# Last feed-forward fed with the un-normalised stream: the factor 1/rms on its gate and up products, the shift as two more moving columns

## The reference

```python
D_MODEL, SEQ, CTX_LEN, DEPTH, D_FF = 1024, 256, 256, 2, 2816

def _rms(x, w):
    return x * lax.rsqrt(jnp.mean(x * x, axis=-1, keepdims=True) + EPS) * w

def _modulate(x, shift, scale):
    return x * (1 + scale[:, None, :]) + shift[:, None, :]

def _swiglu(x, w_gu, w_down):
    g, u = jnp.split(x @ w_gu, 2, axis=-1)
    return (jax.nn.silu(g) * u) @ w_down

for l in range(DEPTH):
    ...
    h = h + 0.5 * m[2][:, None] * _swiglu(_modulate(_rms(h, norm_w[l, 0]), m[0], m[1]), ffn1_w_gu[l], ffn1_w_down[l])
    ...
    h = h + m[5][:, None] * y          # y: the mixer's output
    h = h + 0.5 * m[8][:, None] * _swiglu(_modulate(_rms(h, norm_w[l, 2]), m[6], m[7]), ffn2_w_gu[l], ffn2_w_down[l])
return h                               # the latent stream alone
```

## Time and profile before

| | |
|---|---|
| median of 3 runs | 1715.92 us (1715.57 to 1716.11) |
| the profiled execution, its own time | 1716.46 us |
| its span on the core | 1714.7 us |
| TensorE matmul busy | 1664.4 us, 97% |
| VectorE busy | 1085.4 us, 63% |
| ScalarE busy | 609.5 us, 36% |
| mean granted TensorE clock | 0.993 |

### The profile page before, as it was taken

One profiled execution on the slowest core, in us unless ns is written; L12 is line 12 of the kernel. 1 busy time (PEld: TensorE's weight loads), 2 busy tenths in 40 slices (PEclk: granted clock), 3 DMA queues, 4 the chain that ended last, 5 costly groups with the idle time before them and its releaser, 6 DMA issues.

```text
span 1714.7 us, 23714 instructions
## 1 busy us (share of the span) xinstructions
PE 1664.4 (97%) x9475; PEld 1412.5 (82%) x9475; DVE 1085.4 (63%) x1652; ACT 609.5 (36%) x917; POOL 85.0 (5%) x150
## 2 busy tenths in 40 slices
PE   3999999999999999999999999999999999979999
PEld 1888888889767898888888898888888987979999
DVE  2777787636668567777773368777523587655543
ACT  2422222124645452222222252222222365444432
POOL 0000000000000100000000000000000000000000
PEclk9999999999999999999999999999999999989999
DMA  9255555532211224555552235555323232435554
GB/s 365 96 187 190 180 195 179 191 111 75 99 62 50 87 87 163 183 195 179 190 188 97 83 101 195 183 185 187 134 97 98 87 111 74 139 116 182 183 169 148
DMA packets 69882, 249.42 MB, mean 145 GB/s; under 512 B 7441, under 2 KB 8465, under 8 KB 69777
## 3 DMA queue, kind: packets, MB, share of 16 engines
q1 hardware_dynamic: 51344, 180.83, 31.7%
q0 software_dynamic: 18432, 67.12, 11.7%
HBM read 246.87 MB, written 1.05 MB: 145 GB/s over the span
## 4 chain that ended last, share of the span: by engine, by line
PE 93%; DVE 2%; DMA 1%; SPq 1%; issue 1%; ACT 1%; POOLq 0%; POOL 0%; DVEq 0%; ACTq 0%
PE ps L1168 30%; PE ps L1169 29%; PE ps L1170 29%; DMA raw<-wstream 1%; PE ps L1229 1%; PE ps L1371 1%; PE ps L1403 1%; ACT whi L398 1%; PE ps L1331 1%; DVE wlo L685 1%; SPq L328 1%; SPq L324 0%; PE ps L1385 0%; DVE nmax L1013 0%; PE ps L1412 0%
## 5 line engine op out<-in xcount | busy, mean ns | idle before, releaser
L685 DVE TENSOR_TENSOR wlo<-raw,whi 128x1024 fp32r<-128x1024 f32 x320 | 393.7, 1230 | 546.8 <-ACT whi L398 545.9
L1168 PE MATMUL ps<-xh,whi 128*128 128x512 f32 (+1 forms) x1956 | 690.2, 353 | 8.5 <-DVE xl L795 5.1
L1169 PE MATMUL ps<-xl,whi 128*128 128x512 f32 (+1 forms) x1956 | 674.3, 345 | 0.0
L1170 PE MATMUL ps<-xh,wlo 128*128 128x512 f32 (+1 forms) x1956 | 673.7, 344 | 0.0
L398 ACT ACTIVATE whi<-raw 128x1024 fp32r<-128x1024 f32 x320 | 338.6, 1058 | 897.5 <-PE ps L1170 764.2
L1168 PEld LDWEIGHTS ps<-xh,whi 128*128 128x128 f32 x1956 | 372.3, 190 | 65.7 <-issue 12.0
L1169 PEld LDWEIGHTS ps<-xl,whi 128*128 128x128 f32 x1956 | 372.6, 190 | 45.7 <-issue 3.8
L1170 PEld LDWEIGHTS ps<-xh,wlo 128*128 128x128 f32 x1956 | 372.2, 190 | 44.7
L710 DVE SCALAR_TENSOR_TENSOR shared_a<-wm,cs,shared_a 128x512 f32<-128x512 f32 x448 | 307.6, 747 | 0.0
L1168 PE MATMUL ps<-ah,whi 128*128 128x512 f32 (+1 forms) x800 | 274.9, 344 | 3.7 <-DVE shared_b L733 3.7
L1169 PE MATMUL ps<-al,whi 128*128 128x512 f32 (+1 forms) x800 | 273.0, 341 | 0.0
(11 more groups left out here) (106 smaller groups left out, 797.5 us busy)
## 6 DMA issues: line engine op xcount, KB each, us to landing
raw<-wstream SPq DMA_DIRECT2D x320, 512.0 KB, 3.5
wm<-wmod POOLq DMA_DIRECT2D x128, 512.0 KB, 4.7
wm<-wmod SPq DMA_DIRECT2D x3, 2048.0 KB, 21.0
h<-x_t SPq DMA_DIRECT2D x1, 2048.0 KB, 11.9
wm<-wmod SPq DMA_DIRECT2D x2, 1024.0 KB, 20.4
out_t<-h SPq DMA_DIRECT2D x8, 128.0 KB, 2.6
K<-cols SPq DMA_DIRECT2D x1, 939.0 KB, 13.8
K<-cols SPq DMA_DIRECT2D x1, 268.5 KB, 3.0
```

The costliest lines, as they stand in the source:

```text
L685: dve.tensor_tensor(wlo[:, n % RING, :, :].rearrange("p a b -> p (a b)"), raw[:, n % RING, :], whi[:, n % SPL, :, :].rearrange("p a b -> p ...
L1168: pe.matmul(out_ap, hi_w, hi_x, start=start, stop=False)
L1169: pe.matmul(out_ap, hi_w, lo_x, start=False, stop=False)
L1170: return pe.matmul(out_ap, lo_w, hi_x, start=False, stop=stop)
```

## The change

Only the last feed-forward and what feeds it change. Since rms^-1 is one factor per token, (x * a * r + s) W = r * (x * a) W + s W. So:

- ScalarE and VectorE make the high and low part of `h * acol`, without the norm's factor, chunk by chunk as the output projection's chunks are added to `h` (`high_last`, `low_last`). They are stored in rows of 512 fp32 (2048 bytes) where the attention's buffers were (`xh_last`, `xl_last`), and columns 256 and 257 of each row hold the shift (of the latent and of the context stream; only the first is used).
- Gate and up matmuls move 258 columns instead of 256. Their first three blocks go chunk by chunk together, with the sum of squares (`norm_stat`) ahead of the last chunk.
- Per hidden chunk ScalarE copies the two shift products out of PSUM (`srow`), VectorE multiplies gate and up by rms^-1 into SBUF in one instruction of 2x256 (`gu_last`, semaphore `gu_scaled`), ScalarE takes silu with the shift product as bias, and VectorE does (up + shift product) * silu. TensorE may overwrite the banks after `gu_scaled`.
- The first half of the down blocks uses banks 4, 6, 7, 5, the second half banks 0 to 3.
- In the output projection VectorE does the update ahead of the split of weights, and the last split of it after `low_last`.

```diff
+XW = S + 2
...
+        rstd_last = shared_b[:, T + S:2 * T]
+        gu_last = af[:, :, S:T]
...
+        xh_last = ah[:, 0:DC * T].rearrange("p (c t) -> p c t", c=DC)
+        xl_last = ah[:, DC * T:2 * DC * T].rearrange("p (c t) -> p c t", c=DC)
+        ah_last = al[:, FC * S:2 * FC * S]
+        al_last = al[:, 0:FC * S]
...
+            def high_last(d):
+                act.wait_ge(h_done, h_count(4, d, 0))
+                act.activation(xh_last[:, d, 0:S], h[:, d, 0:S], ACT.Identity, scale=acol[:, 5, d, 0:1]).then_inc(ha_hi, 1)
+
+            def ffn_last():
...
+                for j in range(FC):
+                    split_next(n0 + 2 * j)
+                    if j:
+                        hidden_high(f, j - 1, w)
+                    b = 2 * j % 4
+                    act.wait_ge(block_done, n0 + 2 * j + 2)
+                    if j >= 2:
+                        act.wait_ge(mul_done, F0 + j - 1)
+                    act.activation(srow[:, j % 2, :, 0:1], ps[:, b:b + 2, S:S + 1], ACT.Copy).then_inc(srow_done, 1)
+                    split_next(n0 + 2 * j + 1)
+                    act.wait_ge(gu_scaled, j + 1)
+                    act.wait_ge(srow_done, j + 1)
+                    act.wait_ge(mul_done, F0 + j - 1)
+                    act.activation(sil[:, j % 2, 0:w], gu_last[:, 0, :], ACT.Silu, bias=srow[:, j % 2, 0, 0:1])\
+                        .then_inc(silu_done, 1)
...
-                    for d in range(JOINT, DC):
-                        split_next(n0 + OQ + d)
-                        square(m, d)
-                    root(m, 0)
+                    for d in range(DC):
+                        split_next(n0 + OQ + d)
+                        high_last(d)
+                        square(m, d)
...
             # VectorE
+            def low_last(d):
+                dve.wait_ge(ha_hi, d + 1)
+                dve.scalar_tensor_tensor(xl_last[:, d, 0:S], h[:, d, 0:S], acol[:, 5, d, 0:1],
+                                         xh_last[:, d, 0:S].bitcast(F32), ALU.mult, ALU.subtract).then_inc(ha_lo, 1)
...
+                    split_next(n0 + 2 * j)
+                    if j:
+                        hidden_low(f, j - 1, w)
...
+                    dve.wait_ge(srow_done, j + 1)
+                    dve.tensor_tensor(gu_last, ps[:, b:b + 2, 0:S], rows, ALU.mult).then_inc(gu_scaled, 1)
+                    split_next(n0 + 2 * j + 1)
+                    dve.wait_ge(gu_scaled, j + 1)
+                    dve.wait_ge(silu_done, F0 + j + 1)
+                    dve.scalar_tensor_tensor(af[:, j % 2, 0:w], gu_last[:, 1, :], srow[:, j % 2, 1, 0:1],
+                                             sil[:, j % 2, 0:w], ALU.add, ALU.mult).then_inc(mul_done, 1)
...
+                for d in range(DC):
+                    dve.wait_ge(block_done, n0 + OQ + d + 1)
+                    update(m, d, d % 4)
+                    if d:
+                        low_last(d - 1)
+                        add_square(m + 1, d - 1)
+                    if d < DC - 1:
+                        split_next(n0 + OQ + d)
+                low_last(DC - 1)
+                split_next(n0 + OQ + DC - 1)
...
             # TensorE
+                for q in range(FIRST):
+                    pe.wait_ge(lo_done, n0 + q + 1)
+                for c in range(DC):
+                    if c == DC - 1:
+                        norm_stat(m)
+                    pe.wait_ge(ha_lo, c + 1)
+                    if c == 0:
+                        pe.wait_ge(h_done, h_count(4, JOINT + FIRST - 1, 0))
+                    for q in range(FIRST):
+                        ins = chunk_last(n0 + q, q, c)
...
+                for b in range(FIRST, GU):
+                    if b % 2 == 0:
+                        pe.wait_ge(gu_scaled, b // 2 - 1)
+                    pe.wait_ge(lo_done, n0 + b + 1)
+                    for c in range(DC):
+                        ins = chunk_last(n0 + b, b % 4, c)
```

More of the change, by code:

```diff
@@ L431, in ffn @@
                     split_next(n0 + GU + b)
[L432 to L435, removed]
+                for d in range(JOINT):
+                    square(m + 1, d)
+                ln_exp_tables()
                 nd = n0 + GU + HALF
@@ L438, in ffn @@
                     split_next(nd + b)
[L439 to L443, removed]
+                boundary(m + 1, nd + HALF)
+            def high_last(d):
+                act.wait_ge(h_done, h_count(4, d, 0))
+                act.activation(xh_last[:, d, 0:S], h[:, d, 0:S], ACT.Identity, scale=acol[:, 5, d, 0:1]).then_inc(ha_hi, 1)
+            def ffn_last():
+                f, w = 3, S
+                F0 = FC * f
+                n0 = PER_LAYER + FFN + MIX
+                for j in range(FC):
[13 more added lines that the diff above has]
+                        .then_inc(silu_done, 1)
+                hidden_high(f, FC - 1, w)
+                for b in range(DN - TAIL):
+                    split_next(n0 + GU + b)
             def ln_exp_tables():
@@ L738, in hidden_low @@
                 dve.wait_ge(ah_done, FC * f + j + 1)
-                dst = slice(j * T, j * T + w)
-                dve.tensor_tensor(al[:, dst], af[:, j % 2, 0:w], ah[:, dst].bitcast(F32), ALU.subtract)\
-                    .then_inc(al_done, 1)
+                dst = slice(j * T, j * T + w) if f < 3 else slice(j * w, (j + 1) * w)
+                high, low = (ah[:, dst], al[:, dst]) if f < 3 else (ah_last[:, dst], al_last[:, dst])
+                dve.tensor_tensor(low, af[:, j % 2, 0:w], high.bitcast(F32), ALU.subtract).then_inc(al_done, 1)
             def gate_columns(m):
@@ L892, in ffn @@
                     split_next(nd + b)
[L893 to L904, removed]
+                dve.wait_ge(block_done, nd + HALF - TAIL)
@@ L1203, in first_blocks, with chunk_last, ffn_last, down @@
                     column_block(n + 2, FIRST_BANKS[m][2], a, b, last)
+            def chunk_last(n, bank, c):
+                return three(ps[:, bank, 0:XW], whi[:, n % SPL, c, :], wlo[:, n % RING, c, :],
+                             xh_last[:, c, 0:XW], xl_last[:, c, 0:XW], c == 0, c == DC - 1)
+            def ffn_last():
+                f, m, w = 3, 5, S
+                n0 = PER_LAYER + FFN + MIX
+                pe.wait_ge(shift_lo, 1)
+                for q in range(FIRST):
[8 more added lines that the diff above has]
+                        ins = chunk_last(n0 + q, q, c)
+                        if c == DC - 1:
+                            ins.then_inc(block_done, 1)
+                pe.wait_ge(h_done, h_count(4, DC - 1, 0))
+                for b in range(FIRST, GU):
[4 more added lines that the diff above has]
+                        ins = chunk_last(n0 + b, b % 4, c)
+                    ins.then_inc(block_done, 1)
+                def down(hf, b, order, parts=0):
+                    n = n0 + GU + HALF * hf + b
+                    banks = DN_BANKS[1 - hf]
+                    pe.wait_ge(lo_done, n + 1)
+                    for r, d in order:
+                        src = (2 * b + r) * w
+                        ins = three(ps[:, banks[d], 0:w], whi[:, n % SPL, 4 * r + d, :],
+                                    wlo[:, n % RING, 4 * r + d, :], ah_last[:, src:src + w], al_last[:, src:src + w],
+                                    b == 0 and r == 0, b == HALF - 1 and r == 1)
+                        if r == 1 and d < parts:
+                            ins.then_inc(part_done, 1)
+                    ins.then_inc(block_done, 1)
+                by_row = [(r, d) for r in range(2) for d in range(4)]
+                by_bank = [(r, d) for d in range(4) for r in range(2)]
+                pe.wait_ge(rstd_done, 2 * m + 1)
+                for b in range(HALF):
+                    pe.wait_ge(al_done, FC * f + 2 * b + 2)
+                    down(0, b, by_row)
+                pe.wait_ge(gu_scaled, FC)
+                for b in range(HALF - 1):
+                    down(1, b, by_row)
+                down(1, HALF - 1, by_bank, parts=3)
@@ L1299, in ffn @@
                     pe.wait_ge(mod_rows, f + 1)
[L1300 to L1304, removed]
                 main = HALF - TAIL
```

93 lines of the change are left out of this document (67 added, 26 removed).

## The result

The changed kernel takes 1705.98 us, median of 4 runs (1704.70 to 1706.85), against 1715.77 before; ratio 0.9942, 95% interval 0.993 to 0.9955. That is 9.8 us less where 17 were forecast, and 2.5 us above the range.

What follows compares the result with a forecast made beforehand. TensorE, busy 97% of the span, was taken as the bound. Of 20.6 us lost there, new losses of 1.3 + 0.7 + 0.7 + 0.9 = 3.6 leave 17.0 less: 1699.2 us forecast, range 1696.2 to 1703.5.

Steps and rivals of the forecast that it cites:

- signs of being wrong: 258-column matmuls more than 2 ns from 256-column ones, shared_b as releaser chunk after chunk, or a low clock behind 1502.
- Start of the feed-forward: Behind the last output projection: TensorE stops 1.2 us instead of 12.6, waiting for weight block 256, and restarts 0.1 slower.
- The sum of squares: Now inside the matmul stream ahead of the last chunk: costs 0.7 us; no slow clock expected, gain 2.7.
- First reuse of banks: Ahead of blocks 258 and 260: waits of 0.3 and 0.2 us, with two restarts 0.7 in all, against 1.0 before.
- Two columns more: Gate/up matmuls of 258 columns: 0.83 ns more each on a line from 256 to 512, 0.9 us over 1056.
- Steady gate/up: Per hidden chunk VectorE needs 3.9 us and ScalarE about 2.9, hidden behind TensorE's 5.8: no cost.
- The rival of a dearer width: Gate/up: 258 columns cost far more than two columns; charged as 32 more 1712.5 us, chance 0.03; slower (1754), 0.05.
- The rival of a chain at every chunk: Gate/up: scaling makes VectorE and ScalarE a chain TensorE waits for each chunk; +10 us, 1709; chance 0.05.
- Down: Between gate/up and down: the 2.6 us stop and the slow clock's 1.6 go; the later half costs 0.
- Rivals 3 and 4: Stop ahead of down stays, 1703.5 us, chance 0.05; start waits longer because splits come late, 1703, chance 0.10.

Runs made afterwards that it cites:

- gap128_in_before: The kernel before with only an unused tile of 128 bytes a partition added ahead of shared_a; 1720.56 us, ratio 1.0031.
- srow_no_shift: The changed kernel with srow as a piece of the dead tile mrows, so every other buffer lies as in the kernel before; 1699.96 us, ratio 0.9908.
- no_shift_256_columns: As srow_no_shift, but gate and up matmuls move 256 columns, shift products left out and column 0 read in their place; 1698.49 us, ratio 0.9903.
- banks_swapped_in_before: The kernel before with only the last feed-forward's down blocks taking banks 4, 6, 7, 5 first, 0 to 3 later; 1711.78 us, ratio 0.9977.
- update_first_in_before: The kernel before with only VectorE's update of h ahead of the weight split in the last output projection, last split behind the norm; 1708.19 us, ratio 0.996.

## Why the prediction was wrong

**The step that failed** is none of the terms, but what stood under them: that outside the listed parts the kernel stays as it is. "From the profiled execution 1716.46 - 17.0" carries all that stands ahead of 1501 over unchanged, as does "I set SyncE's issues up to 1501.4 as before": a cost put at nothing, without a reason. The new tile `srow` moved `ah` and `al` against the weights by 128 bytes, and 1296 matmuls of 512 columns in the three earlier down stretches cost 5.6 to 6.1 ns more each. With what the 256-column ones of these stretches give back that is 7.1 us. The full diff has it (`srow = sb(...)` ahead of `shared_a`), the lines of it that I showed leave it out, and no rival of mine had it. gap128_in_before shows the cause with nothing else changed, and srow_no_shift that the rest of the sum holds: 1700.0 for 1699.2. Of the signs of being wrong that the prediction names, one came: 258 columns are 2.2 ns dearer than the 120.0 of 256 before, and 3.5 dearer than the 118.7 of 256 beside them. It pointed at the columns, which are not where most of the miss lay.

Point by point, in the changed kernel:

- *Start of the feed-forward*: 1.2 us and a restart were forecast, set by weight block 256. The row of 1508.46 names `wlo` as releaser and the gap is 1.23 us (1507.23 to 1508.46). Right; part of it is the chance of one execution, since the gap is 1.47 in srow_no_shift and 0.7 to 1.5 in the four kernels made from it, with the same order of work.
- *The sum of squares*: 0.68 us from 1516.23 to 1516.91. Right. The clock stayed at 1.00.
- *First reuse of banks*: 0.7 us forecast for two stops; they were 0.1 each with 0.1 for each restart, 0.4. The first scaling is ready at 1521.1 and the second at 1527.2, which are the 1514.9 to 1515.1 and the 1521.1 worked out plus the 6.0. The chains were sized right; TensorE itself came 0.2 to 0.3 later to both, in part because its 258-column matmuls were dearer, and so waited less. In srow_no_shift the second stop is 0.46. Right in place, small in size. The two scalings on VectorE, and ScalarE ahead of the second:

```profile
1520.42 0.68 DVE L965 TENSOR_TENSOR shared_b<-ps,shared_b 128x512 f32<-128x512 f32 x1
1526.47 0.69 DVE L965 TENSOR_TENSOR shared_b<-ps,shared_b 128x512 f32<-128x512 f32 x1
...
1521.13 1.06 ACT L414 ACTIVATE whi<-raw 128x1024 fp32r<-128x1024 f32 x1 [1.90 <-DMA raw<-wstream]
1522.21 1.28 ACT L480 ACT_TABLE_LOAD   x1
1523.51 0.51 ACT L480 ACTIVATE shared_b<-shared_b,srow 128x256 f32<-128x256 f32 x1
```

The table load takes 1.28 us; it starts 0.02 behind the split ahead of it, and the next operation 0.02 behind it. The Trainium skill ("ScalarE: Activation LUTs", What ACT_TABLE_LOAD costs) has 2.66 us with a drain; there is none of it here, the measurement decides.

- *Two columns more*: 0.83 ns on the line is what they cost with the rows at distance 0 (no_shift_256_columns). At 128 bytes they cost 2.2 ns, 1.4 us more than forecast; the 256-column down gave back 528 x 1.3 ns = 0.7. The rival of a dearer width had the right sign but not the reason: the price of a width depends on the placement.
- *Steady gate/up*: VectorE is busy 25.5 of 40 us, 3.7 a chunk (3.9 forecast); behind block 260 TensorE waits nowhere. The rival of a chain at every chunk did not come.
- *Down*: no stop, no low clock. By itself, in banks_swapped_in_before, it is worth 3.9 us of the 4.2.
- *Rivals 3 and 4* did not come.

What stays open: why the distance matters. The runs show that it is counted from the weight tiles, since moving those along undoes it and leaving them alone brings it on, and that 256, 512 and 1024 bytes act as 0 does. They also show one distance, 128 bytes, with two paces for 256 columns. The Trainium skill ("TensorE: Matmul & The Clock Gate", Step-by-step: what each phase is for) says that loading the next weights takes no SBUF read bandwidth from the running matmul. No run here shows what the two reads do to each other. That the pace depends on where the one operand lies from the other fits badly with reads that are fully independent; a conflict between them would fit, but that is not shown.

## What to carry to other kernels

Read a diff for what it allocates as well as for what it runs: a small tile put ahead of others moves them all, and the matmul pace depended on it here by 3% (512 columns) to 6% (256). Where TensorE is the bound, put new tiles behind the matmul operands or into dead ones, and compare the start-to-start times of matmuls that the change should not touch: that separates such a cost from the change. And split a wait into its order and its data: moving one instruction ahead of another on VectorE was 7 of the 12.6 us, at no cost in arithmetic. Try such reorderings by themselves first: here they gave more than the algebra did.

## What the runs showed of the hardware that was not expected

- The start-to-start time of a matmul with its own weight load at full clock depends on the distance between moving rows and weights modulo 256 bytes: 113.3 to 120.0 ns for 256 columns, 118.7 to 122.2 for 258, 226.7 to 233 for 512. What is best for one width is not for another: 128 bytes are good for 256 columns (in most stretches) and bad for 258 and 512.
- The distance that packs nicely, 0, is the slowest measured for 256 columns. With 192 bytes the 528 down matmuls take 3.5 us less (528 x 6.7 ns, in one run).
- How long the low clock lasts behind a stop is not set by the length of the stop alone: it was low for 6 us of work behind 12.6 us in the kernel before and for 3.7 us behind the same stop in gap128_in_before (3.3 behind 5.6 us in update_first_in_before). Stops of 1.0 to 1.5 us brought none.
- At the level of 1.2 GHz (1514 to 1520 in the kernel before) 256 columns take 0.213 us from start to start, which is 256 / 1.2 GHz, with nothing over; at 2.4 GHz 13 ns more than the columns alone.
